# Another order of the query blocks in the attention of a hybrid decoder trunk

## The reference

```
sc  = q_block @ k.T                      # 128 queries against the keys 0 .. 128*(block+1)-1
sc  = where(key <= query, sc, -big)
p   = softmax(sc)                        # over the keys
out = p @ v                              # 128 x 64
```

## Time and profile before

| what | value |
|---|---|
| median of 3 runs | 2354.04 us (2353.93 to 2354.62) |
| the profiled execution | 2356.05 us, its span 2354.3 us |
| TensorE | 2278.9 us busy, 97% of the span |
| VectorE, ScalarE, GpSimd | 1337.1, 903.4, 1034.3 us busy |
| chain that ended last | TensorE 87%, VectorE 7%, ScalarE 3%, issue 2% |

### The profile page before, as it was taken

One profiled execution on the slowest core, in us unless ns is written; L12 is line 12 of the kernel. 1 busy time (PEld: TensorE's weight loads), 2 busy tenths in 40 slices (PEclk: granted clock), 3 DMA queues, 4 the chain that ended last, 5 costly groups with the idle time before them and its releaser, 6 DMA issues.

```text
span 2354.3 us, 31829 instructions
## 1 busy us (share of the span) xinstructions
PE 2278.9 (97%) x10415; PEld 1853.0 (79%) x10415; DVE 1337.1 (57%) x2177; ACT 903.4 (38%) x1595; POOL 1034.3 (44%) x715
## 2 busy tenths in 40 slices
PE   6999999999999999999989999999999999999997
PEld 5786777778888888888868878878788888888885
DVE  7755555248755555555681115663875555555556
ACT  4535554124433333333441114451433333333333
POOL 3413333333555555555433332224335555555554
PEclk9998999999999999999999999999999999999998
DMA  4100000311111111111231110012011111111112
GB/s 166 45 27 1 1 0 28 117 36 45 36 54 49 50 51 48 53 53 54 58 125 59 45 45 28 27 65 88 28 36 54 54 54 49 49 53 46 53 54 90
DMA packets 34583, 122.07 MB, mean 52 GB/s; under 512 B 3840, under 2 KB 3968, under 8 KB 34240
## 3 DMA queue, kind: packets, MB, share of 16 engines
q1 hardware_dynamic: 31328, 105.39, 14.5%
q10 hardware_dynamic: 3168, 15.54, 1.7%
HBM read 112.52 MB, written 8.39 MB: 51 GB/s over the span
## 4 chain that ended last, share of the span: by engine, by line
PE 87%; DVE 7%; ACT 3%; issue 2%; POOL 0%; DMA 0%; ACTq 0%; DVEq 0%; POOLq 0%; SPq 0%
PE ps L808 10%; PE ps L806 10%; PE ps L810 10%; PE ps L728 8%; PE ps L730 8%; PE ps L729 8%; PE ps L846 6%; PE ps L847 6%; PE ps L848 6%; PE ps L1575 2%; PE ps L1722 1%; PE ps L1726 1%; PE ps L1724 1%; PE ps L1563 1%; PE ps L603 1%
## 5 line engine op out<-in xcount | busy, mean ns | idle before, releaser
L509 POOL TENSOR_TENSOR wlo<-stage,whi 128x512 fp32r<-128x512 f32 x308 | 397.5, 1296 | 461.6 <-ACT whi L971 457.2
L728 PE MATMUL ps<-ahi,whi 128*128 128x512 f32 x896 | 368.7, 412 | 29.8 <-POOL wlo L434 19.1
L427 POOL TENSOR_TENSOR whi<-stage,cons 128x1024 fp32r<-128x1024 f32 x64 | 125.7, 1965 | 525.9 <-PE ps L730 311.5
L730 PE MATMUL ps<-ahi,wlo 128*128 128x512 f32 x896 | 351.0, 392 | 0.0
L729 PE MATMUL ps<-alo,whi 128*128 128x512 f32 x896 | 350.7, 391 | 0.0
L1231 DVE TENSOR_TENSOR hT<-hT,ps 128x512 f32<-128x512 f32 x352 | 238.8, 686 | 161.2 <-PE ps L848 161.2
L971 ACT CAST whi<-stage 128x512 fp32r<-128x512 f32 x308 | 189.1, 620 | 364.6 <-POOL stage L522 180.9
L846 PE MATMUL ps<-hid_hi,whi 128*128 128x512 f32 x640 | 252.3, 394 | 2.1 <-DVE hT L1231 1.5
L848 PE MATMUL ps<-hid_hi,wlo 128*128 128x512 f32 x640 | 249.6, 390 | 0.0
L847 PE MATMUL ps<-hid_lo,whi 128*128 128x512 f32 x640 | 249.6, 390 | 0.0
L806 PE MATMUL ps<-ahi,whi 128*128 128x512 f32 x608 | 236.7, 389 | 0.0
(11 more groups left out here) (323 smaller groups left out, 4095.3 us busy)
## 6 DMA issues: line engine op xcount, KB each, us to landing
stage<-in_wt SPq DMA_DIRECT2D x184, 512.0 KB, 3.6
hT<-in_xt SPq DMA_DIRECT2D x16, 256.0 KB, 9.6
hT<-in_xt ACTq DMA_DIRECT2D x8, 512.0 KB, 7.8
spill<-hT ACTq DMA_DIRECT2D x1, 4096.0 KB, 12.1
hT<-spill ACTq DMA_DIRECT2D x8, 512.0 KB, 8.4
out<-hT SPq DMA_DIRECT2D x16, 256.0 KB, 2.1
wqb_s<-in_wqb ACTq DMA_DIRECT2D x1, 1024.0 KB, 4.9
wlru_s<-in_wlru ACTq DMA_DIRECT2D x1, 512.0 KB, 6.4
```

What stands on the lines that cost most here:

```text
L509: nc.gpsimd.tensor_tensor(block_lo(c), src, block_hi(c).bitcast(F32), ALU.subtract).then_inc(sem(L + "b_ready"), 1)
L728: nc.tensor.matmul(bank, hi, rhs_k[0][:, tok], start=k_first, stop=False)
L730: return nc.tensor.matmul(bank, lo, rhs_k[0][:, tok], start=False, stop=k_last)
```

## The change

The list of the blocks is another one, and the two places at which TensorE waits for the split queries of the next head move with it: `scores` now waits in the steps 0 and 1 of a head (before in 0 and 2), and in the very first head step 0, which is block 7, waits for three of the four parts and step 1, which is block 0, for all four.

```
-        order = [6, 7, 0, 1, 4, 5, 2, 3]
+        order = [7, 0, 6, 1, 5, 2, 4, 3]
...
             def scores(h, par, k, step):
 
                 qt = order[k]
-                if k in (0, 2):
-                    pe.wait_ge(sem("qk_lo"), h * 4 + (3 if isinstance(step, int) and step < 2 else 4))
+                if k < 2:
+                    pe.wait_ge(sem("qk_lo"), h * 4 + (3 if isinstance(step, int) and step == 0 else 4))
```

## The result

The changed kernel took 2380.29 us (median of 5 runs, 2377.06 to 2382.47) against 2353.96 (2353.77 to 2354.62) for the kernel before: a ratio of 1.0107, 95% interval 1.0096 to 1.0118, or 26 us more. Its profiled execution took 2381.54 us with a span of 2379.7, against 2356.05 and 2354.3. The forecast was 2374.0 us, with a range of 2363 to 2383.

The account below looks back on a forecast made before the run. The attention's head loop was taken as bound by TensorE, with about 7% of waits. Waits of 15.5 us plus clock 5.6 gave 21.1, rounded down to +20 on 2354.0: 2374.0 us, range 2363 to 2383.

Parts of the forecast that it names:

- The end of a head: Weighing of block 3 waits for ScalarE's copy behind block 7's exponentials: 1.6 us where 0.68 stood, +0.92 a head.
- P2: Projection part 2 on TensorE, waiting for VectorE's rotation of part 1: +0.8 us a head, no wait before.
- P1: Projection part 1 on TensorE, waiting for VectorE's rotation of part 0: 0.78 us left uncovered, +0.55 us a head.
- W4: Weighing of block 4, mid-head: its 0.36 us wait goes, block 2's weighing may wait instead; -1.5 us in all.
- The second go: Turns of every second head: the wait for VectorE grows by 0.45 us, three times, +1.4 us (0 to +2.1).
- The third go: Turns of every second head: the 0.53 us wait for the output shrinks by up to 0.15, four times, -0.5 us.
- The clock: TensorE's clock also falls at the ends of heads 0, 2, 4 and 6: 5.6 us, bounds 0 and 14.
- The third rival: Clock falls also at the second go or behind P1 and P2: five more falls, +7, 2381 us; 19%.
- the first: Rival: the clock falls no more often than before, waits only, +15.5 us, 2369.5 us; 25%.
- The second: Rival: smaller rotation waits, end of a head at its low end, clock as before: about +8, 2362 us; 10%.
- The fourth: Rival: faster, ScalarE's work per step more even, so copy waits and three clock falls go: -12, 2342 us; 4%.
- The fifth: Rival: nothing moves, because the order is hidden behind another bound; 2%.

Follow-up runs that it names:

- the filled changed kernel: Changed kernel with three matmuls without use ahead of the weighing in step 7 of every head, one ahead of each third go: 2367.64 us, ratio 1.0052.
- the filled kernel before: Kernel before with one matmul without use ahead of the weighing in step 7 of every head, one ahead of each third go: 2355.16 us, ratio 0.9999.
- the fill: Matmuls without use put into TensorE's waits at the ends of heads: 2367.64 us on the changed kernel, 2355.16 us on the kernel before.

## Why the prediction was right, and where it was not

**The three waits.** The end of a head: forecast 1.6 us where 0.68 stood, measured 1.57 in six heads and 1.67 in the seventh. P2: 0.8 forecast, 0.84 to 0.86 measured. P1: 0.78 forecast, 0.62 to 0.63 of idle matmul time, up to 0.8 on the weight loads; more of TensorE's work lay beside the same 2.99 us than my 2.21. These are the steps on which the direction rested, and each stood where it was said, with the releaser that was said.

**The middle and the turns.** W4's 0.36 went and W2's 0.16 came, in every second head only: forecast -1.5, measured -1.9. The second go waits 1.00 instead of 0.78, +0.2 each and not +0.45. The third go kept its 0.53: the -0.15 did not come. The last head was lighter by 1.2 us of idle, against -0.5; in the second trace of the changed kernel, where the clock is up there, W0 waits 0.70 us that this trace does not show, and the difference is 0.5. The first exponentials wait 2.44 us instead of 0.17, most of it scores of block 7 that moved out of the way: the loop's first transposes started 5.4 us after the first scores and 5.3 before, so +0.1 where I put +0.7.

**Waits together.** Forecast 15.5, measured 32.7 - 16.2 = 16.5 us of idle time. That sum is right, but it is not yet the waits' share of the time: the 2.3 us more ahead of the first transposes cost 0.1, and 1.9 us of waits at P0 stood hidden behind the slow clock before, which leaves 12.4. At full clock head pairs can be compared in the two kernels with filled waits. From P1 to P1 the filled changed kernel takes 27.4 us for an even head and 30.1 for an odd one (starts 304.10 and 334.17 for the odd). From W4 to W4 the filled kernel before takes 25.3 and 28.9. That is +2.1 in four heads and +1.2 in three, 12 us, and 12.5 lie between the two medians, 2367.64 and 2355.16. The odd heads are cheaper than my 2.2 us, because at full clock the kernel before waits 0.56 to 0.72 at P0 and the changed one, with the long T7 and S6 there, does not. I had not seen that wait, since the slow clock hid it in the one profile I had.

**The clock, the term that was mis-sized.** "4 x 1.4 = 5.6 us" assumed one fall of 3.4 us behind every head that had none. The number of falls was not the error: six of the seven ends of heads had one where three had before, so three more and not four. The error was the length. Behind the heads 1 and 2 the clock stayed down for 6.8 us and behind head 6 for 10.2, against 3.4 each time behind the heads 1, 3 and 5 before, and each cost by its length: from P1 to P1 these heads took 32.9 instead of 30.1 us, and 30.5 instead of 27.4. My count also left out a stretch of 6.8 us at the end of the last head before (from 422.4 us), which the changed kernel's trace does not have.

The lengths are those of one execution. In the second trace of the changed kernel, with the same waits, they are 6.8, 3.4, none, 3.4, 3.4, 3.4 and none behind the heads 0 to 6, and 10.2 us from 441.3 us on, behind the second go of the last head. What decides how long the clock stays down was not found. Its price is better read from the fill: it took 10.4 us off the changed kernel and 0 off the kernel before. So the 26.3 us (22.9 on another chip) are about 12 of waits and 10 to 14 of clock, not 15.5 and 5.6. My waits were too dear by some 3 us and my clock too cheap by 5 to 8. The two errors went opposite ways, so that the median came out only 6.3 us over the forecast owes something to luck.

The third rival (falls also at the second go or behind P1 and P2, 2381 us) named the right size for the clock, but the wrong place in the profiled execution: its slow stretches from 215 us on all begin at the ends of heads. In the second trace the one from 441.3 us begins behind a second go, and in the order 4 7 6 5 1 0 2 3 all four between 215 and 420 us begin at the goes. It was this rival that carried the range up to 2383.

Against the rivals: the first (waits only, 2369.5) falls by the fill. The second (rotation waits small) falls by the rows. The fourth (faster, since ScalarE's work is more even) falls too; its point of decision was whether the chain to W3 is shorter than the work beside it, and it is 3.5 against 1.9 us. That the steps are even on one engine did not help, because the wait is set by how much of TensorE's work stands beside a chain. The fifth (nothing moves) falls by the interval, 1.0096 to 1.0118.

In the Trainium skill, "TensorE: Matmul & The Clock Gate", section "A second HAM failure mode: psum-queue depth-cycling", short idle times between groups of matmuls make the clock go back and forth. The slow stretches after waits of at most 1.7 us agree. The end of head 4, and six of seven ends of heads with 1.08 us of idle in the order 7 6 0 1 4 5 2 3, had no fall and do not. The price that the page puts on it, lost throughput beside the idle time, agrees with what the fill gave back.

## What to carry to other kernels

In a hand-made pipeline, price a new order step by step: the chain through the other engines from its releasing instruction to the waiting one, less the bottleneck engine's work that stands between them. Most of the waits so priced came out within 0.2 us here, also for orders that had not been run (W3 1.2 forecast and 1.08 measured, then 0.15 to 0.3 forecast and none measured). The largest surprises were waits that nobody had priced: W0 behind the rotation, P0 behind a pair, the later goes. Then price TensorE's clock apart, with a range: in the changed kernel it cost about as much again as the waits, and matmuls without use inside a wait show how much it is. A profile with falls of the clock can hide waits that show once the falls are gone. A wait taken away can come back through another semaphore behind the same instruction, so look for all who wait for it.

## What the runs showed of the hardware

The same idle time at the ends of the heads (1.57 us, at the last of them 1.67) was followed by slow stretches of 3.4, 6.8, 6.8, 3.4, none, 3.4 and 10.2 us in one execution, and of 6.8, 3.4, none, 3.4, 3.4, 3.4 and none in another. With 1.08 us there, one end of seven had a fall. The changed kernel's runs spread over 5.4 us and those of before over 0.9 beside them, but in the experiments the kernel before spread over 5.2 us (23 runs), 7.3 (16) and 5.7 (13), so the spread is no mark of the change. Matmuls without use (six trace entries in 1.4 us at the end of a head) went with a clock of 1.00 from 215 us to the loop's end, and cost nothing where they fit into a wait.
